# Sparse attention inside a decoder layer: another order of the query tiles, and score runs that start in a buffer still being read

## What is computed

```python
s_c = q @ kcmp - slopes * dist_c                  # 127 compressed keys
p_c = softmax(where(mask_c, s_c, NEG_INF)) * mask_c
imp = p_c @ overlap                               # importance of 32 blocks of 64 keys
_, sel_idx = top_k(where(forced, FORCE_SCORE, imp), 8)
s  = q @ ks[sel_idx] - slopes * dist              # selected blocks
p  = softmax(where(dist >= 0, s, NEG_INF));  o_sel = p @ vs[sel_idx]
sw = q @ kw[window of 512] - slopes * dw          # sliding window
pw = softmax(where(mw, sw, NEG_INF));        o_win = pw @ vw
o = gate0 * o_cmp + gate1 * o_sel + gate2 * o_win
```

## Time and profile before

| | us |
|---|---|
| median of 3 runs | 4533.3 (4529.51 to 4541.09) |
| the profiled execution | 4524.15 |
| its span, first to last instruction | 4522.4 |
| main part of the attention in it, 1735.5 to 2778.5 | 1043.0 |
| mean granted clock of the span | 0.932 |

### The profile page before, as it was taken

How to read it: one execution, slowest core, us unless ns; L and a number is a source line. 1 busy time by engine, 2 the same in 40 slices (tenths; PEclk the granted TensorE clock), 3 DMA queues, 4 the chain that set the end, 5 groups by cost and what they waited for, 6 DMA issues and landing times. The chain is left out here.

```text
span 4522.4 us, 69615 instructions
## 1 busy us (share of the span) xinstructions
PE 3997.7 (88%) x26720; PEld 3236.5 (72%) x26721; DVE 2442.8 (54%) x4140; ACT 1986.3 (44%) x3138; POOL 547.3 (12%) x849
## 2 busy tenths in 40 slices
PE   7899999999989857888888876899779999999698
PEld 5677777777767635666667665799658888887587
DVE  2544455454455425677667644444477445567465
ACT  2433333433332214655556643322146555566465
POOL 1101121111121102111111110200111000001110
PEclk9999999999998968999999976899879999999899
DMA  4443443433332250000000002434369666689542
GB/s 133 131 108 100 126 113 89 127 99 81 105 84 75 65 115 24 15 12 15 13 15 20 20 17 69 159 115 133 116 238 349 237 225 223 227 336 344 218 149 92
DMA packets 512950, 557.20 MB, mean 123 GB/s; under 512 B 106284, under 2 KB 374572, under 8 KB 511628
## 3 DMA queue, kind: packets, MB, share of 16 engines
q1 hardware_dynamic: 471476, 457.94, 31.9%
q0 software_dynamic: 16416, 59.78, 3.5%
q10 hardware_dynamic: 24784, 35.71, 2.4%
HBM read 439.78 MB, written 113.57 MB: 122 GB/s over the span
## 5 line engine op out<-in xcount | busy, mean ns | idle before, releaser
L525 PE MATMUL fr_fb<-fr_hT_h,fr_w_h 128*128 128x512 f32 (+1 forms) x1312 | 539.5, 411 | 7.8 <-DVE fr_hT_r L979 6.2
L525 PE MATMUL fr_fb<-fr_hT_r,fr_w_h 128*128 128x512 f32 (+1 forms) x1312 | 537.4, 410 | 0.0
L525 PE MATMUL fr_fb<-fr_hT_h,fr_w_r 128*128 128x512 f32 (+1 forms) x1312 | 536.6, 409 | 0.4 <-issue 0.4
L959 DVE TENSOR_TENSOR fr_w_r<-fr_w_raw,fr_w_h 128x1024 fp32r<-128x1024 f32 (+1 forms) x164 | 198.0, 1208 | 522.3 <-ACT fr_w_h L775 521.3
L1886 DVE TENSOR_TENSOR aq_p_lo<-aq_t_bank,aq_p_hi 128x512 fp32r<-128x512 f32 x412 | 281.3, 690 | 268.8 <-ACT aq_p_hi L1776 267.5
L1776 ACT CAST aq_p_hi<-aq_t_bank 128x512 fp32r<-128x512 f32 x412 | 238.8, 585 | 375.3 <-PE aq_t_bank L1690 373.2
L799 ACT COPY fr_zs<-fr_fb 128x512 f32<-128x512 f32 (+1 forms) x148 | 87.1, 589 | 508.4 <-PE fr_fb L525 508.0
L525 PEld LDWEIGHTS fr_fb<-fr_hT_h,fr_w_h 128*128 128x128 f32 (+1 forms) x1312 | 252.1, 192 | 74.0 <-issue 11.0
L525 PEld LDWEIGHTS fr_fb<-fr_hT_h,fr_w_r 128*128 128x128 f32 (+1 forms) x1312 | 251.9, 192 | 64.7 <-issue 11.0
L525 PEld LDWEIGHTS fr_fb<-fr_hT_r,fr_w_h 128*128 128x128 f32 (+1 forms) x1312 | 252.5, 192 | 63.2 <-issue 9.6
L134 PE MATMUL ex_gu<-wx_gate_w,ex_xT 128*128 128x512 f32 x1176 | 288.3, 401 | 4.8 <-DVE ex_xT L2642 4.7
(11 more groups left out here) (474 smaller groups left out, 8819.7 us busy)
## 6 DMA issues: line engine op xcount, KB each, us to landing
wx_raw<-in_w_exp_gate_up SPq DMA_DIRECT2D x64, 2048.0 KB, 10.3
fr_w_raw<-in_w_in SPq DMA_DIRECT2D x160, 512.0 KB, 3.9
wx_raw<-in_w_exp_down SPq DMA_DIRECT2D x32, 2048.0 KB, 10.8
s_z<-fr_zs SPq DMA_DIRECT2D x160, 256.0 KB
s_rows<-ex_y ACTq DMA_DIRECT2D x50, 512.0 KB, 4.3
mx_mg<-s_z SPq DMA_DIRECT2D x32, 512.0 KB, 7.7
fr_zc<-s_z SPq DMA_DIRECT2D x15, 903.0 KB, 6.8
fr_x_t<-in_x SPq DMA_DIRECT2D x16, 512.0 KB, 5.3
```

What stands on the lines that cost most here:

```text
L525: ins = pe.matmul(bank[0:cols_, :], (w_h, w_h, w_r)[p][:, k, c, 0:cols_].bitcast(F32R), (hT_h, hT_r, hT_h)[p][:, c, :].bitcast(F32R), star ...
L959: dve.tensor_tensor(w_r[:, m % 2, :, 0:cols_].bitcast(F32R), w_raw[:, m % 2, :, 0:cols_], w_h[:, m % 2, :, 0:cols_], ALU.subtract).then_in ...
```

## The change

The 16 tiles are taken in an order that is written out as a table: 15, 14, 13, 12, then 3, 11, 2, 10, 1, 9, 0, 8, then 7, 6, 5, 4. Everything that used the tile's number for its place in the order (buffers, waits, loads) now uses its index in this table. The last but one selected unit, which stands in the 640-column buffer, is now S(4,0), which has just 640 columns.

A selected unit of t of 8 and more (`reused`) now gets its first run in the step in which the first 1024 columns of the buffer have been turned by the selected unit two units earlier; the first halves of all four heads come first, then the second halves, no earlier than the turns that free their columns. DVE's waits follow. Where the earlier selected unit has fewer blocks than that, the runs begin with its last step. The front's "out" stands at least 7 steps ahead of these runs. No instruction of the computation is added or taken away.

```diff
+    TILES = (15, 14, 13, 12, 3, 11, 2, 10, 1, 9, 0, 8, 7, 6, 5, 4)
+    Y_RING, FRONTS_APART, TABLE_STEPS = 3, 7, 7
...
-            runs = [(h, at, min(RUN, width - at)) for h in range(Q_PER_KV) for at in range(0, width, RUN)]
+            runs = [(h, at, min(RUN, width - at)) for at in range(0, width, RUN) for h in range(Q_PER_KV)]
+            begin, end = self.begin[u], f[u] - 2
+            if self.reused(u + 1):
+                end = min(end, self.begin[u + 1])
             for i, (h, at, wide) in enumerate(runs):
-                step = f[u - 1] + i * max(f[u] - f[u - 1] - 2, 1) // len(runs) if u else -1
+                step = begin + i * max(end - begin, 1) // len(runs)
+                if self.reused(u):
+                    step = max(step, f[u - 2] + self.blocks_over(u, at + wide) - 1)
...
-            later = min(f[self.at[t, g, SEL] - 1] - 4, later - self.FRONTS_APART)
+            u = self.at[t, g, SEL]
+            later = min(self.begin[u] - (self.TABLE_STEPS if self.reused(u) else 4), later - self.FRONTS_APART)
...
-            pool += [(out - 4, 0, n, "normalise", t, g), (f[self.at[t, g, SEL] - 1], 1, n, "bias", t, g)]
+            pool += [(out - 4, 0, n, "normalise", t, g), (self.begin[self.at[t, g, SEL]] - 2, 1, n, "bias", t, g)]
...
+    def reused(self, u):
+        return 5 <= u < len(self.units) and self.units[u][2] == self.units[u - 2][2] == SEL and self.units[u][0] >= RUN // P
+
+    def first_run(self, u):
+        f = self.first
+        if not u:
+            return -1
+        return f[u - 2] + self.blocks_over(u, RUN) - 1 if self.reused(u) else f[u - 1]
+
+    def blocks_over(self, u, columns):
+        return min(columns // P, self.first[u - 1] - self.first[u - 2])
...
-                        dve.wait_ge(turned, F.first[u - 1])
+                        dve.wait_ge(turned, F.first[u - 2] + F.blocks_over(u, at + wide) if F.reused(u) else F.first[u - 1])
...
-                        dve.wait_ge(s_read, i)
+                        dve.wait_ge(s_read, i - R + 1)
```

More of the change, by code:

```diff
@@ L1243 @@
 class Plan:
[L1247 removed]
+    TILES = (15, 14, 13, 12, 3, 11, 2, 10, 1, 9, 0, 8, 7, 6, 5, 4)
+    Y_RING, FRONTS_APART, TABLE_STEPS = 3, 7, 7
     def __init__(self):
[L1250 removed]
+        pairs = [(t, g) for t in self.TILES for g in range(KV_HEADS)]
         ahead = 2
@@ L1265, in __init__ @@
         f = self.first
-        self.runs_at, self.run_end = {}, []
+        self.runs_at, self.run_end, self.begin = {}, [], []
+        for u in range(len(self.units)):
+            self.begin.append(self.first_run(u))
         total = 0
@@ L1312, in __init__ @@
         for t, g in pairs:
-            if t + self.Y_RING < NT:
-                assert self.misc["turn_y", t + self.Y_RING, 0] < min(self.misc["out", t, g], self.misc["back", t, 2 * g + WIN])
+            if self.TILES.index(t) >= self.Y_RING:
+                assert self.misc["turn_y", self.before(t, self.Y_RING), 0] < min(self.misc["out", t, g], self.misc["back", t, 2 * g + WIN])
     def low(self, u):
```

40 lines of the change are left out of this document (20 added, 20 removed).

## The result

The changed kernel is a little slower: 4548.5 us (median of 16 runs) against 4529.3 for the one before, ratio 1.0046 with an interval of 1.0033 to 1.0059.

A forecast was written before the change was run, and what follows sets the result against it. No single engine bounds the kernel: PE limits selected units, DVE's masks and then an exponential the windows. Terms -2 - 40 - 10.6 + 7 - 25 - 19 + 40 gave -50 us, a median of 4483 us, range 4443 to 4550.

The forecast's parts named there:

- Tiles 15 to 12: Tiles 15 to 12: window units lose 30 us, selected units take over score runs and grow by 28; net -2 us.
- Windows of 11 to 8 and of 7: Window units of tiles 11 to 7: fewer or narrower score runs, -40 us for 11 to 8, -10.6 for 7.
- Selected units of 11 to 8: Selected units of tiles 11 to 8: group 0 grows by 11.6 us, group 1 loses 4.3 of half clock; +7 us.
- Short units: The 16 units of tiles 3 to 0, now between long ones: 172.0 us before, 147 after; -25 us.
- The end: Last units: S(4,0) and S(4,1) get faster, tiles 7 to 5 and W(4,.) lose some 10 us; -19 us.
- The clock: Main part: some eight PE idles behind exponentials bring half clock, 5 us each; +40 us, bounds 0 and 80.
- The table: DVE's early masks wait for POOL's table of chosen blocks: covered, 0 us; otherwise up to 3 us per unit.
- (b): Rival, slower: DVE and PE take turns; masks at whole price +36, short units no cheaper +25, clock +40; chance 0.14.

The follow-up runs named there:

- e2: The kernel before plus the early score runs alone, tiles left descending: ratio 0.9949, 4504.5 us, main part 1027.4 us.
- e1: The changed kernel with its new tile order alone, score runs placed as before the change: ratio 1.0073 to the kernel before, main part 1091.5 us.
- e3: The changed kernel plus three unused PE matmuls behind each exponential of a long selected unit: ratio 1.0084 to the kernel before, main part 1097.7 us.
- e4: The kernel before plus three unused PE matmuls behind each exponential of a long selected unit: ratio 0.9996, main part 1045.9 us.
- h1: Descending tiles with early score runs, but all eight runs of S(11,0), S(10,0), S(9,0), S(8,0) on one step: ratio 1.0032 to the kernel before, main part 1064.2 us.

## Why the prediction was wrong

The sum said -50 us, -90 for its parts and +40 for the clock; the main part came out at +30.7, the medians at +19. The measured parts below have the clock in them. **Steps 3 and 4 are where it failed most**, by 31 and 35 us; step 5 missed by 26, steps 1 and 2 by 12 each. By its steps:

1. **Tiles 15 to 12** (-2 forecast). Right in the mechanism, the work moves from one to the other, and too hopeful in both sizes: the windows lost 24.4 us (89.6 to 65.2; forecast 30), the selected units grew by 34.9 (forecast 28), 8 of it in S(15,0), which ran at 0.86. Net +10.5, and +16 in e2: here the early runs don't pay. The three windows ahead of these, which the sum left out, took 3.8 more.
2. **Windows of 11 to 8 and of 7** (-40 and -10.6). 136.0 to 106.8 and 37.6 to 28.5: -29.2 and -9.1. Right in kind; most of the windows are at 9 to 12 us; W(10,1) and W(9,1) took 16.6 and 17.2 at clocks of 0.73 and 0.64, W(11,0) 16.5 at 0.90.
3. **Selected units of 11 to 8** (+7). This is the first step that failed. They went from 166.2 to 204.0 us, **+37.8**. I gave the four units of group 0 11.6 us for the runs of group 1 that they take over. But a window of one or two steps takes none of them, so S(10,0) and S(9,0) hold eight each in their last steps, four on one step, and grew by 11 and 13; group 0 grew by 30.1. And the group-1 units, which I had shrinking by 4.3, grew by 7.7. The sum also took the fronts of the short tiles off the units of tiles 7 to 5 (-10, step 5) and put them, with the short tiles' backs, nowhere: against e2, more of the growth of S(10,0) and S(9,0) lies in the first three steps, where these stand, than in the last.
4. **Short units** (-25). This failed too. 172.1 to 182.4: **+10.3**. The couples were worked out as 24, 22, 19 us and came to 28.9, 26.7 and 27.4, with S(0,1) at 11.2 instead of 4.5. I had the runs on one step in this sum, with eight masks of 8.5 us and 6 us of idle PE; what I left out is that PE's turns stand behind all eight runs, so that the casts and remainders that I laid beside the masks come after them (ACT idle 10.86 us), and that each heap is paid again in the unit behind it. S(1,1) has PE's 6.16 us for `take_q` besides, which the sum doesn't have.
5. **The end** (-19). S(4,0) and S(4,1) 30.3 to 18.5, as forecast. The units of tiles 7 to 5 with W(4,0) and W(4,1) did not lose 10 us but rose from 181.2 to 199.8: W(5,0) 12.2 to 17.1 at a clock of 0.80, W(4,0) 20.0 to 23.3 at 0.66. Why just these rose is not settled: they were at 183.7 in e2 and at 191.5 in e1, so that it comes with the order of the tiles.
6. **The clock** (+40). 67 us more at half clock (165 to 232), so at most 34 us, already counted in the parts above. e3 and e4 show 1 to 3 us for a fall in a unit of some 20 to 30 us, with up to 2.8 us of filler working against it, so that my 5 us for a fall are neither shown nor ruled out. The clock in the main part went from 0.92 to 0.89. That it falls was right; it can't be what turned -50 into +31, since 34 is less than the 40 in the sum.
7. **The table**: 0 us for DVE's masks, as forecast. These are the masks that read `aq_tg`, over the main part of the kernel after (x count | busy us, mean ns | idle before, by releaser); POOL is the releaser of none of their waits. What I missed is `take_q`, which stands behind the table in POOL's queue:

```profile
L1902 DVE CUSTOM_DVE_ANT_0 aq_sc_odd<-aq_s_bank,aq_tg 128x1024 f32<-128x1024 f32 (+7 forms) x124 | 120.7, 990 | 10.8 <-PE aq_s_bank L1727 6.7 <-DVE aq_y L1838 3.8 <-PE aq_t_bank L1714 0.3
...
L1902 DVE CUSTOM_DVE_ANT_0 aq_sc_odd<-aq_s_bank,aq_tg,aq_least 128x1024 f32<-128x1024 f32 (+7 forms) x64 | 50.4, 810 | 3.5 <-PE aq_s_bank L1727 2.3 <-DVE aq_y L1868 0.4 <-PE aq_t_bank L1714 0.4
```

Of the rivals, (b) had the sign and one of its three parts (short units no cheaper). Its first part, masks at their whole price of 7.2 us in every selected unit, came in S(15,0) alone (+7.0 in e2); the six units of tiles 15 to 13 grew by 4.5 each there. The forecast's error is that it priced the tile order by the steps of the short units and treated the runs of the long ones, and the short tiles' events, as work that finds cover somewhere. That S(10,0) and S(9,0) have all their runs on one step can be read from the order of the instructions alone; h1 prices such a step at 9 us.

## What to carry to other kernels

Where one engine's queue carries both a chain that feeds the others (turn, cast, remainder) and bulk work for a later unit, count how many steps of the chain the bulk work has to lie beside: eight runs on one step cost 9 us more here than the same eight on six to eight steps. Interleaving short units with long ones takes those steps away just where the next long unit's work is due. When a change has two parts, price and run them apart: here one was worth -16 to -23 us and the other +33 to +48, and in the second the traces show waits for a queue (POOL's) and for a bank's events that the sum didn't look at.
